# Interleaving gate columns, a row spread and the chunk transposes with the contraction steps of three in-projection tiles

## The reference

```python
p = rmsnorm(h, g_mix) @ w_in                 # 560 tokens x 1024  @  1024 x 2720
qkv, z, b, a, c_q, c_kv, k_pe = split(p)     # 1536, 512, 8, 8, 384, 256, 32 columns
qkv_c = silu(causal_conv(qkv, conv_w))       # depthwise, width 4
q, k, v = heads(qkv_c);  q, k = l2norm(q) * 64**-0.5, l2norm(k)
beta = sigmoid(b);  g = -exp(a_log) * softplus(a + dt_bias)
# gated delta rule in chunks of 16 tokens (4 for samples): g = cumsum(g) within a chunk
decay = exp(g_i - g_j)                       # i >= j
A     = I + strict_lower(k_beta k^T * decay) # solved by substitution
qk    = lower(q k^T * decay)
# then one step per chunk:  v_new = u - w S;  o = q e^g S + qk v_new;  S = S e^gl + k_dec^T v_new
```

## Time and profile before

| what | value |
|---|---|
| three executions, median | 1118.54 us |
| the profiled execution's own time | 1116.36 us |
| its span, first to last instruction | 1114.6 us |
| mean granted TensorE clock | 0.962 of full speed |
| PE busy, share of the span | 1022.3 us, 92% |
| DVE, ACT, POOL busy | 48%, 39%, 15% |
| instructions | 20673 |

### The profile page before, as it was taken

One profiled execution on the slowest core, in us unless ns is written; L12 is line 12 of the kernel. 1 busy time (PEld: TensorE's weight loads), 2 busy tenths in 40 slices (PEclk: granted clock), 3 DMA queues, 4 the chain that ended last, 5 costly groups with the idle time before them and its releaser, 6 DMA issues.

```text
span 1114.6 us, 20673 instructions
## 1 busy us (share of the span) xinstructions
PE 1022.3 (92%) x8636; PEld 865.4 (78%) x8636; DVE 540.0 (48%) x1084; ACT 430.1 (39%) x873; POOL 164.2 (15%) x258
## 2 busy tenths in 40 slices
PE   3999999999977878889898979999999999999997
PEld 3989889777745534555555559999999999999997
DVE  5555857564478349634443453264334334433433
ACT  6444755655331446433333342353124113213412
POOL 1021300465320200235344100000000000000000
PEclk9999889999589899989999989999999999999999
DMA  6312110300011600256665232132222232232212
GB/s 228 100 58 79 46 33 34 115 5 5 1 37 36 225 21 1 66 191 217 209 229 201 82 114 77 39 133 76 86 104 76 81 109 77 79 111 76 77 39 81
DMA packets 24999, 101.76 MB, mean 91 GB/s; under 512 B 7752, under 2 KB 8568, under 8 KB 18435
## 3 DMA queue, kind: packets, MB, share of 16 engines
q1 hardware_dynamic: 15690, 62.68, 16.8%
q0 software_dynamic: 9216, 37.75, 9.7%
HBM read 96.21 MB, written 4.22 MB: 90 GB/s over the span
## 4 chain that ended last, share of the span: by engine, by line
PE 61%; DVE 8%; ACT 3%; issue 2%; POOL 1%; ACTq 0%; DVEq 0%
PE PS L567 13%; PE PS L565 13%; PE PS L566 13%; PE PS L1008 4%; PE PS L1043 3%; PE PS L1019 2%; PE PS L897 2%; PE PS L1026 2%; ACT PE L1512 1%; DVE SMX L1985 1%; PE PS L1034 1%; PE PS L924 1%; ACT PTE L1525 1%; PE PS L943 1%; POOL CN L2192 1%
## 5 line engine op out<-in xcount | busy, mean ns | idle before, releaser
L565 PE MATMUL PS<-XH,WH 128*128 128x272 f32 (+1 forms) x944 | 277.2, 294 | 3.2 <-DVE WL L1589 1.7
L567 PE MATMUL PS<-XH,WL 128*128 128x272 f32 (+1 forms) x944 | 276.1, 292 | 0.0
L566 PE MATMUL PS<-XL,WH 128*128 128x272 f32 (+1 forms) x944 | 275.2, 292 | 0.0
L565 PEld LDWEIGHTS PS<-XH,WH 128*128 128x128 f32 x944 | 180.1, 191 | 8.3 <-issue 4.2
L566 PEld LDWEIGHTS PS<-XL,WH 128*128 128x128 f32 x944 | 180.2, 191 | 0.0
L567 PEld LDWEIGHTS PS<-XH,WL 128*128 128x128 f32 x944 | 179.9, 191 | 0.0
L1152 ACT ACTIVATE WH<-RAW 128x2048 fp32r<-128x2048 f32 x47 | 89.9, 1913 | 203.9 <-PE PS L567 202.7
L565 PE MATMUL PS<-NH,WH 128*128 128x272 f32 x512 | 149.1, 291 | 0.8 <-DVE WL L1589 0.8
L567 PE MATMUL PS<-NH,WL 128*128 128x272 f32 x512 | 147.6, 288 | 0.0
L566 PE MATMUL PS<-NL,WH 128*128 128x272 f32 x512 | 146.6, 286 | 0.0
L1589 DVE TENSOR_TENSOR WL<-RAW,WH 128x2048 fp32r<-128x2048 f32 x47 | 108.0, 2297 | 63.4 <-ACT WH L1152 63.4
(11 more groups left out here) (313 smaller groups left out, 1518.5 us busy)
## 6 DMA issues: line engine op xcount, KB each, us to landing
RAW<-in_w_stream SPq DMA_DIRECT2D x47, 1024.0 KB, 4.9
XN<-in_hin SPq DMA_DIRECT2D x4, 512.0 KB, 6.7
out_y_p<-YO SPq DMA_DIRECT2D x4, 512.0 KB, 2.7
WQ<-in_wq SPq DMA_DIRECT2D x1, 1536.0 KB, 8.1
CST<-in_big SPq DMA_DIRECT2D x1, 1132.5 KB, 13.3
SS<-in_sstate SPq DMA_DIRECT2D x1, 1024.0 KB, 4.8
out_ssm_s<-SS SPq DMA_DIRECT2D x4, 256.0 KB
CN<-in_cache,IDX POOLq DMA_INDIRECT x64, 6.1
```

The source lines that it names most:

```text
L565: pe.matmul(PS[:, b, 0:n], wh, xh[:, k, c:c + n], start=(k == 0), stop=False)
L566: pe.matmul(PS[:, b, 0:n], wh, xl[:, k, c:c + n], start=False, stop=False)
L567: last = pe.matmul(PS[:, b, 0:n], wl, xh[:, k, c:c + n], start=False, stop=(k == DT - 1))
```

## The change

Three things on PE, one on ACT:

- `gates_to_columns` gets an argument `x` from 0 to 5. Calls 0 to 3 do four of the sixteen strided matmuls each, calls 4 and 5 half of the small ones each; call 0 holds the waits, call 5 posts `pe_step`. They stand inside tile 13, ahead of its k-steps 2 to 7.
- `spread_rows(1)` moves from after tile 12 to after tile 13; `spread_rows(2)` from after tile 13 to inside tile 14, ahead of k-step 3.
- `chunk_transposes(0)` to `(3)` move from after tile 14 to inside tile 15, ahead of k-steps 2 to 5.
- On ACT, at `i` = 13, the decay exponent with its wait stands ahead of `silu_out` instead of behind it.

```diff
-            def gates_to_columns():
+            def gates_to_columns(x):
+                if x == 0:
+                    pe.wait_ge(sem("e16_in"), 16)
+                    pe.wait_ge(sem("dve_step"), DVE_STEP["gates"])
+                    pe.wait_ge(sem("qk_inverted"), 2)
+                    pe.wait_ge(sem("kk_copied"), 2)
-                for t in range(CH):
+                for t in range(4 * x, min(4 * x + 4, CH)):
                     pe.matmul(PS[:, 5, 0:5 * NU], row("e16", t), BROW[:, :, t:T:CH], ...)
-                for p in range(PAIRS):
+                for p in ((0, 1), (2, 3))[x - 4] if x >= 4 else ():
...
-                last.then_inc(sem("pe_step"), 1)
+                if x == 5:
+                    last.then_inc(sem("pe_step"), 1)
...
+            def beside_tile(i, k):
+                if i == 13 and k >= 2:
+                    gates_to_columns(k - 2)
+                elif i == 14 and k == 3:
+                    spread_rows(2)
+                elif i == 15 and 2 <= k < 6:
+                    chunk_transposes(k - 2)
...
-                last = weight_tile(i // 2, i % 2, (XH, XL), (b, b + 1), HALVES)
+                last = weight_tile(i // 2, i % 2, (XH, XL), (b, b + 1), HALVES, lambda k: beside_tile(i, k))
...
-                elif i == 12:
-                    gates_to_columns()
+                elif i == 13:
                     spread_rows(1)
-                elif i == 13:
-                    spread_rows(2)
-                elif i == 14:
-                    for x in range(4):
-                        chunk_transposes(x)
...
+                if i == 13:
+                    act.wait_ge(sem("dve_step"), DVE_STEP["decay_diff"])
+                    act.activation(TMP[:, :, :], TMP[:, :, :], ACT.Exp, scale=-1.0).then_inc(sem("act_step"), 1)
                 if i and TILES[i - 1] < 12:
                     silu_out(CONV.index(TILES[i - 1]))
...
                 elif i == 13:
-                    act.wait_ge(sem("dve_step"), DVE_STEP["decay_diff"])
-                    act.activation(TMP[:, :, :], TMP[:, :, :], ACT.Exp, scale=-1.0).then_inc(sem("act_step"), 1)
                     last_rates()
```

## The result

The changed kernel takes 1121.84 us (median of 16 executions, 1113.77 to 1124.88) against 1117.66 us for the kernel before on the same chip (16 executions, 1109.37 to 1119.90). The ratio is 1.005, 95% interval 1.0027 to 1.0073: slower by 4.2 us. Forecast was 1122.0 us. Neither kernel has one time: five of the 16 executions of the kernel before lie at 1109.4 to 1111.5 us and the others at 1116.4 to 1119.9, while of the changed kernel one lies at 1113.8 and the others at 1118.7 to 1124.9. Between the medians of the upper groups (1118.24 and 1121.85) the difference is 3.6 us.

What follows compares the result with a forecast made beforehand. PE was taken as the bound; gates, k-steps, spreads and transposes, mostly at half clock, ended tile 15 at 174.1 us against 170.61, so 1118.54 + 3.5 = 1122.0 us, range 1112.4 to 1124.2 (8 in 10).

Steps and rivals of the forecast that it cites:

- early return: Rival: clock falls one or two groups later, returns within tile 14's first three k-steps; +0.3 us, 1118.8 us; chance 0.28.
- late return: Likeliest case: clock low through tile 13, back 3.7 us into tile 14's last five k-steps; +3.5 us; chance 0.42.
- gates to the end of tile 13: PE, tile 13: strided passes 9.53 us, small matmuls 3.24, six k-steps at 1.40 each, ending at 152.2.
- second spread: PE, now after tile 13: 2.3 us at half clock, ending at 154.5.
- third spread, five k-steps: PE, tile 14: spread 1.9 us, then five k-steps 5.5 us with the clock returning 3.7 us into them.
- tile 15 with transposes: PE: eight k-steps 6.3 us and 16 transposes 1.7 us, ending at 174.1 against 170.61 before.
- Waits: PE: the 1.97 us wait before the gates shrinks to 0.5; the 1.0 us before the chunk transposes goes.
- The clock: PE, tiles 13 and 14: falls to 0.50 at 132.7 us or one or two groups later, returns only after tile 13.
- The insertions: Small matmuls and transposes between k-steps: priced at 0 beyond their passes; upper bound some 2 us for nine.
- Not a coin toss from run to run: Recurrence behind chunk 26: the later clock fall doesn't vary between executions, since three runs lie within 1 us.
- the clock stays up: Rival: full clock through tile 13, ending at 147.0; 5.8 us earlier, 1112.7 us; chance 0.20.
- Later fall avoided: Rival: recurrence behind chunk 26 stays at full clock, gaining 8 to 9 us; 1113.5 us; chance 0.07.

Runs made afterwards that it cites:

- first profile: The changed kernel, profiled execution beside its timing runs: 1118.74 us, 50.79 us from tile 12 to tile 16 against 47.95 before.
- second profile: The same changed kernel profiled again with no edit: 1123.51 us, 55.24 us from tile 12 to tile 16.
- the gates' part alone: Kernel before with only gates and spreads moved, transposes and exponent as before: 1121.25 us against 1115.96, ratio 1.0044.
- the last experiment: Kernel before with DVE's four index instructions moved from chunk 26 to chunks 20 to 23: 1107.41 us against 1117.77, ratio 0.9929.

## Why the prediction was right

The changed kernel's gates start 8.4 us behind the start of tile 12 in both profiles, and so they did before; from there to tile 16 every step can be laid beside the forecast (us; the steps run from start to start):

| step | forecast | first profile (early return) | second profile (late return) |
|---|---|---|---|
| gates to the end of tile 13 | 21.1 | 23.4 | 23.4 |
| second spread | 2.3 | 2.2 | 2.2 |
| three k-steps | 4.2 | 3.8 | 4.5 |
| third spread, five k-steps | 7.4 | 5.1 | 8.9 |
| tile 15 with transposes | 8.0 | 7.9 | 7.9 |
| sum; less 39.55 as before | 43.0; +3.5 | 42.4; +2.8 | 46.8; +7.3 |

- **Waits: right.** 0.5 us ahead of the gates, none ahead of the transposes, no table load ahead of the exponent. That PE would not wait in tile 15 for lack of ACT's edit was seen as well, in the profile of the gates' part alone, which has the late return.
- **The clock: right.** It fell one group late, did not come back in tile 13, and came back in tile 14, at its beginning or at its end. The forecast had one of these as the likeliest and the other as a rival; three profiles with this order through tiles 13 and 14 show one early return and two late ones. How the 16 executions split, no record says. The late return was at 168.0, 0.5 us ahead of tile 15. The forecast had it after 3.7 us of dense work behind the third spread; it came after 6.2 us (161.77 to 168.0), which costs 1.2 us.
- **The insertions, taken at 0: mis-sized.** Tile 13 was 2.3 us longer than forecast in both profiles. A group of eight strided passes and its k-step should cost 2.37 + 0.77 = 3.14 us at full clock and 2.37 + 1.40 = 3.77 at half; they took 3.49 and 4.34, 0.35 and 0.57 more, and the two groups of small ones 0.48 more each ((153.98 - 146.98 - 6.04) / 2). In the first profile that makes 2.9 us for six insertions; 0.6 came back, since the k-step of the first group still ran at full clock. Four groups with 128-row weights paid nothing, and the transposes, 128 rows too, took 1.21 us with their k-step (166.54 to 167.75), which is four times 0.109 and 0.77. The weight loads point to where the time goes: rows of the changed kernel, whose last 8-row pass starts at about 132.69, 0.30 us behind the 132.39 of the first row.

```profile
132.39 0.76 PE L548 MATMUL PS<-BROW,E 8*128 8x175 f32 x2
133.08 0.19 PEld L567 LDWEIGHTS PS<-XH,WH 128*128 128x128 f32 x1 [0.49 <-issue]
133.19 0.19 PEld L568 LDWEIGHTS PS<-XL,WH 128*128 128x128 f32 x1
...
166.42 0.48 PEld L603 LDWEIGHTS PS<-CST,KK 128*35 128x35 f32 x4
```

  And of the kernel whose strided passes have 128 rows:

```profile
134.44 0.77 PE L549 MATMUL PS<-KQT,CST 128*128 128x175 f32 x2
134.74 0.21 PEld L568 LDWEIGHTS PS<-XH,WH 128*128 128x128 f32 x1
```

  Inside a k-step the weights of line 568 load at 133.19, and its matmul starts at 133.32; the transposes' load stands at 166.42, 0.12 us ahead of 166.54. With 128-row passes the k-step's load begins at 134.74, as soon as the last pass starts (134.44 and 0.30). At the change from 8 to 128 rows it begins at 133.08, together with its own matmul and 0.39 us behind the start of the last pass., on which the 0 rested, has 128-row weights on both sides. So the step of the forecast that was mis-sized is the price of an insertion, taken from rows that don't hold the case; the upper bound, some 2 us for nine insertions, was too small as well, since six took 2.9.
- **The sum came out for two errors that offset.** An early return was put at +0.3 us and was +2.8; a late one at +3.5 and was +7.3. The measured +4.2 (1.0027 to 1.0073 is +3.0 to +8.2 us) is the difference of two medians over executions that differ among themselves, and not the forecast's course at its forecast price. That 1122.0 was met by 0.2 us is luck.
- **"Not a coin toss from run to run": wrong.** The forecast read this from three executions within 1 us. Of all 16 of the kernel before, five lie 5 to 10 us below the other eleven.
- **The rivals.** That the clock stays up is out for this kernel, but its price was sound: with 128-row weights, where it does stay up in tile 13, R is 4.7 us below before (forecast -5.8). Its small matmuls, which the forecast could only bound at full clock, can be read off the run with the block of 128-row passes: three of the four pairs behind it took 1.36 us (139.46 to 140.82), so all four take about 1.8, near the 1.7 used. The Trainium skill, "TensorE: Matmul & The Clock Gate", section "Why this matters for your kernels", had spoken for it: keep TensorE busy and avoid idle gaps. The traces disagree, and they decide: no gap but 0.47 us, PE busy 23.6 us of 23.6, and the clock 0.50. Later fall avoided: it came about in neither profile, and whether it did in the one execution of 1113.8 us is not known; its size is now measured at 8.9 us against the 8 to 9 forecast.

What stays open is why the executions of the kernel before lie in two groups (7 of 19 at 1107.9 to 1111.4 us beside the last experiment, 12 at 1116.5 to 1119.8). With the indices moved, all ten lie at or below 1111.2, which fits that the low group had avoided the later fall. But their median, 1107.41, is 2.9 us below that of the low group, 1110.31, and no profile of an execution of the low group exists.

## What to carry to other kernels

Before small matmuls are put between dense ones to fill a wait, look at the granted clock around them, and not at PE's busy share: if the small ones let the clock fall, keep them in one block, so that as little dense work as possible runs beside them. Filling the wait took 1.5 us of idle time away, but as one block it shortened the stage by only 0.3, and cutting the block into six cost 4.7 to 9.2 (single profiles). And look for the short wait in a sparse stretch: 0.85 us of it cost the recurrence 8.9 us, and moving four index instructions won that back, where the two waits that the change went for held 3.0 us together.

## What the runs showed of the hardware

- Matmuls with 8-row weights neither held nor lifted the clock here, although PE was busy without a gap (23.6 us of 23.6 at 0.50); 128-row ones at the same 0.30 us a pass did both (fallen 130.8, back 134.2, fallen again 141.0 behind 8-row ones, in one kernel).
- A change between 8-row and 128-row weights cost some 0.35 us for going there and back at full clock and 0.57 at half. The traces show with it that the k-step's weight load starts 0.39 us behind the last 8-row pass; with 128 rows on both sides it starts together with the last pass, and the change cost nothing. That the late load is the whole of the cost is argued, not shown.
- A moving operand whose fp32 columns lie 64 bytes apart took nearly twice the time at full clock: 2.51 us for eight passes of 175 columns against 1.38 with runs of 35 neighbours. The Trainium skill, "SBUF — State Buffer", section "Specifications (TRN2)", says that reads that cross to a new 16-byte line pay a penalty; the runs agree.
- The same program's clock returned at 158.9 us in one execution and 168.0 in another. One profile of a kernel whose clock hangs in the balance says little, and several executions are needed.
